# Local attention with a unit of far heads behind every two units of near heads

## The reference

```python
DSWA_CONFIGS = ((128, 1), (512, 4), (2048, 16))
...
def banded_attention(q, k, v, bias, half):
...
    s = jnp.einsum('nbqhe,nbkhe->nbhqk', qb, kw).astype(jnp.float32) * (E ** -0.5)
    s = s + bias[None, None]
...
    s = jnp.where(valid[None, :, None], s, NEG_INF)
    m = jnp.max(s, axis=-1, keepdims=True)
    lse = m + jnp.log(jnp.sum(jnp.exp(s - m), axis=-1, keepdims=True))
    p = jnp.exp(s - lse)
    o = jnp.einsum('nbhqk,nbkhe->nbqhe', p.astype(v.dtype), vw).reshape(N, lp, H, E)[:, :L]
```

## Time and profile before

| | |
|---|---|
| median of 3 runs | 3214.66 us (3212.36 to 3215.52) |
| the profiled execution, its time | 3219.06 us |
| its span | 3217.3 us |
| busy share of the span | PE 94%, PEld 76%, DVE 52%, ACT 34%, POOL 37% |
| mean granted clock of TensorE | 0.967 of full speed |
| the windows stage in the trace | first matmul at 1059.05 us, last copy ends at 1126.70 us: 67.65 us, 2.1% of the span |
| the blending stage behind it | from 1127.48 us |

### The profile page before, as it was taken

The page is one execution under the profiler, slowest core; times in us unless marked ns, Lnnn a source line. Parts: engine busy times, 40 slices in busy tenths (PEclk is TensorE's granted clock), DMA queues, the critical chain, the costliest instruction groups (busy, mean ns, idle before and its releaser), DMA issues. The chain is left out here.

```text
span 3217.3 us, 49457 instructions
## 1 busy us (share of the span) xinstructions
PE 3035.2 (94%) x18790; PEld 2429.6 (76%) x18790; DVE 1671.4 (52%) x2481; ACT 1092.6 (34%) x1740; POOL 1194.3 (37%) x603
## 2 busy tenths in 40 slices
PE   8978988999999889999898999999999979999998
PEld 6855767888878677888487788888888545589987
DVE  7755654321131535311676766555556666478731
ACT  4423433222231632122321342222233435345632
POOL 3432213444444034444122032222323147646643
PEclk9989989999999989999899999999999989999999
DMA  4216453322223022222212111111111112122222
GB/s 147 91 67 233 151 169 115 102 95 94 98 93 117 13 72 96 94 98 95 84 60 74 34 58 63 65 59 65 59 66 59 51 37 50 39 79 93 109 95 85
DMA packets 80058, 275.47 MB, mean 86 GB/s; under 512 B 9484, under 2 KB 12236, under 8 KB 79147
## 3 DMA queue, kind: packets, MB, share of 16 engines
q1 hardware_dynamic: 79627, 273.21, 25.5%
q10 hardware_dynamic: 288, 0.30, 0.0%
HBM read 263.48 MB, written 2.12 MB: 83 GB/s over the span
## 5 line engine op out<-in xcount | busy, mean ns | idle before, releaser
L223 POOL TENSOR_TENSOR weights_low<-weight_ring,weights_high 128x1024 fp32r<-128x1024 f32 x329 | 828.6, 2519 | 1486.5 <-ACT weights_high L217 1422.5
L217 ACT ACTIVATE weights_high<-weight_ring 128x1024 fp32r<-128x1024 f32 x343 | 361.5, 1054 | 784.0 <-PE bank L302 759.0
L300 PE MATMUL bank<-ffn_in_high,weights_low 128*128 128x512 f32 (+2 forms) x1144 | 388.5, 340 | 1.8 <-POOL weights_low L223 1.4
L301 PE MATMUL bank<-ffn_in_low,weights_high 128*128 128x512 f32 (+2 forms) x1144 | 388.2, 339 | 0.0
L302 PE MATMUL bank<-ffn_in_high,weights_high 128*128 128x512 f32 (+2 forms) x1144 | 388.0, 339 | 0.0
L300 PEld LDWEIGHTS bank<-ffn_in_high,weights_low 128*128 128x128 f32 x1144 | 216.5, 189 | 27.1 <-POOL weights_low L223 1.6
L301 PEld LDWEIGHTS bank<-ffn_in_low,weights_high 128*128 128x128 f32 x1144 | 216.5, 189 | 24.2
L302 PEld LDWEIGHTS bank<-ffn_in_high,weights_high 128*128 128x128 f32 x1144 | 215.6, 188 | 23.8
L713 DVE TENSOR_TENSOR mlp_down_low<-mlp_hidden,mlp_down_high 128x512 fp32r<-128x512 f32 x64 | 48.2, 756 | 284.9 <-ACT mlp_down_high L632 284.7
L300 PE MATMUL bank<-mlp_down_high,weights_low 128*128 128x512 f32 x496 | 192.9, 389 | 0.0
L301 PE MATMUL bank<-mlp_down_low,weights_high 128*128 128x512 f32 x496 | 192.9, 389 | 0.0
(11 more groups left out here) (769 smaller groups left out, 7214.3 us busy)
## 6 DMA issues: line engine op xcount, KB each, us to landing
weight_ring<-in_mod SPq DMA_DIRECT2D x96, 512.0 KB, 4.8
weight_ring<-in_ffn_up SPq DMA_DIRECT2D x88, 512.0 KB, 3.3
weight_ring<-in_mlp_up SPq DMA_DIRECT2D x64, 512.0 KB, 3.2
weight_ring<-in_mlp_down SPq DMA_DIRECT2D x64, 512.0 KB, 3.2
weight_ring<-in_ffn_down SPq DMA_DIRECT2D x44, 512.0 KB, 3.3
weight_ring<-in_gdn_in SPq DMA_DIRECT2D x32, 512.0 KB, 3.2
weight_ring<-in_dswa_in SPq DMA_DIRECT2D x27, 512.0 KB, 3.2
weight_ring<-in_fh_in SPq DMA_DIRECT2D x16, 512.0 KB, 3.2
```

What stands on the lines that cost most here:

```text
L217: act.activation(self.high[:, (g.s0 + at) % SPLIT, 0:g.floats], raw, ACT.Copy).then_inc(self.high_ready, 1)
L223: pool.tensor_tensor(self.low[:, slot, 0:g.floats], self.ring[:, (g.c0 + at) % RING, 0:g.floats], self.high[:, slot, 0:g.floats], ALU.subt ...
L300: pe.matmul(bank, wl, ah, start=start, stop=False)
L301: pe.matmul(bank, wh, al, start=False, stop=False)
```

## The change

The list of units is built in another order: two near units, then one far unit, six times over. The first group is (0,0,0), (0,0,1), (1,0), the last is (0,2,2), (0,2,3), (2,2). The list of tiles follows the order in which units first use them, where before it was written out.

```diff
-    units = [(0, i, qb) for i in range(GT) for qb in range(4)] + [(gi, i, None) for gi in (1, 2) for i in range(GT)]
+    near, far = [(0, i, qb) for i in range(GT) for qb in range(4)], [(gi, i, None) for gi in (1, 2) for i in range(GT)]
+    units = [unit for n, one in enumerate(far) for unit in (*near[2 * n:2 * n + 2], one)]
     U = len(units)
-    tiles = [(gi, i) for gi in range(3) for i in range(GT)]
+    tiles = list(dict.fromkeys(unit[:2] for unit in units))
```

## The result

The changed kernel takes 3220.47 us in the median of 19 runs (3217.40 to 3225.05), where the kernel before took 3213.42 in 19 runs beside it. The ratio is 1.0017, with a 95% interval of 1.0011 to 1.0023. It is slower by 5.5 us by the ratio (3.5 to 7.4) and 7.05 us by the medians. A second comparison of the same two kernels gave 1.0016 (1.0008 to 1.0025).

The account below looks back on a forecast made before the run. TensorE was taken as bound, full in the stage's middle and idle only at its ends. Order 5.4 plus clock 1.1 made +6.5 us on the 3214.66 median: 3221.2 us, with 8 in 10 from 3216 to 3228.

Parts of the forecast that it names:

- No work added or removed: In the stage: the change adds and removes no instruction; each engine's work and the bytes moved stay.
- The waits: TensorE ahead of far turns waits for ScalarE's copy behind the far exp: 0.8 and 1.85 us alternately, 2.7 at the first.
- The chain between far scores: From one far unit's scores to the next through VectorE, ScalarE and TensorE: 10.3 us, or 10.8 with the 384-wide neighbour.
- The stage at full clock: The changed stage: start 2.0, middle 53.0 and end 13.3 us, together 68.3.
- The end: From the sixth far unit's scores to the stage's last out copy: 13.3 us.
- The old order at full clock: The stage before the change, 67.65 us less 4.7 of low-clock loss: 62.95, so the order alone costs 5.4.
- The clock: TensorE's low-clock loss in the stage: the old 4.7 us kept, plus 1.1 for two chances in three of another low stretch.
- the clock gives back 3.1 us: Rival: far scores fill the stage's old start gap, keeping full clock; 5.4 - 3.1 = +2.3 us, 3217.0; 26%.
- The rival that was not slower: Near and far units fill each other's gaps, no wait if the far exp were 1.85 us shorter or earlier: 3209.6 us; 7%.
- Low clock in half of the groups: Rival: TensorE's clock low in half of the stage's groups or more, +9 on 5.4: +14 us, 3229, up to 3238; 12%.
- the forecast's border between slower and the same: For the whole kernel, 0.2% (6.4 us) from no change, at 3221.1 us, right at the forecast.
- the 18 us: If transposes don't count as busy for TensorE's clock: low in most groups, about +18 us on top of 5.4; small chance.

Follow-up runs that it names:

- e2: The old order (near units, then far) with each far exp as one 512-column instruction per head, parts of maxima and sums left out: 3210.68 us, ratio 0.9986.
- e10: The changed kernel run again unaltered, beside the kernel before on the same chip: 3220.90 us against 3214.95, ratio 1.0016.
- e11: The changed kernel plus unused identity transposes filling TensorE's wait ahead of all six far turns: 3218.58 us, ratio 1.0011 to the kernel before.
- e1: The changed kernel with each far exp as one 512-column instruction per head, parts of maxima and sums left out: 3208.15 us, ratio 0.9980 to the kernel before.
- e4: On top of e3, ScalarE does each unit's exp one unit later: 3212.48 us, ratio 0.9994 to the kernel before.
- e3: The changed kernel with the turn three units behind the scores instead of two, weighing four, four score slots: 3221.32 us, ratio 1.0019 to the kernel before.
- e5: The changed kernel with units ordered 8 near, 6 far, 4 near: 3211.13 us, ratio 0.9984 to the kernel before.
- e6: The changed kernel plus 20 unused identity transposes ahead of the first far turn: 3217.38 us, ratio 1.0009 to the kernel before.

## Why the prediction was right

- **No work added or removed.** TensorE ran 504 matmul records in the stage in both profiles, ScalarE 190 and VectorE 90. Right.
- **The waits.** Forecast 0.8 and 1.85 us in turn and 2.7 at the first; measured 0.89, 1.67, 0.89, 1.66 and 2.52. The sums of TensorE's list were off by 0.1 to 0.2, the mechanism right.
- **The chain between far scores.** Forecast 10.3 and 10.8 us, measured 10.38 and 10.80 at full clock, with the links as forecast.
- **The stage at full clock.** Forecast 68.3; 68.27 and 68.29 in the two runs that kept full clock. The end was forecast at 13.3 and took 13.22. The old order at full clock was put at 62.95. No run had exactly this, but it can be put together from stretches at full clock: e2's start up to the first far scores (25.85 us), from there to the last turn as in the kernel before (1087.83 to 1119.63, 31.80 us), and e2's end from its last turn on (5.51 us). That makes 63.2. The order's own cost is thus 5.1 us, forecast 5.4.
- **The clock** was the term that was mis-sized. I kept the old loss of 4.7 us and added 1.1. The changed kernel lost 2.8 in its profile and 3.7 in its second one, where 5.8 was forecast. The profile of before lost 4.5 (67.65 less 63.2), which is why the two profiled stages differ by only 3.4 us. I took its loss as the usual one. That execution was 4.4 us above its median, and two of three profiles with this start kept the clock there. An estimate from the medians says the same: 5.1 for the order plus 2.3 of low clock in the changed kernel (e10 less e11) less the 5.5 to 7.05 measured leaves 0.4 to 1.9 us of low clock for the kernel before. So the loss was put too high for both kernels, and the two errors cancel in the difference: +6.5 forecast, +7.05 by the medians, 5.5 by the ratio. That the total came out this close is in part luck. It also lies at the forecast's border between slower and the same: the ratio's interval lies above 1, so the kernel is slower, but it takes in the 0.2% of that border.
- **The rivals.** That the clock gives back 3.1 us was half right at the first waits, as the place of the loss moved from 1065 to behind the first far turn and did not vanish. The rival that was not slower named the far exp as the point of decision, and e1 shows the sign changing there: with 1.43 us the new order wins. Low clock in half of the groups did come in part: it touched two of the five distances between far scores in the first profile, and three and the stage's end in the second. But it cost 2.8 and 3.7 us and not 9, since each time only the turn and the weighing behind the wait ran slow, for 1.2 to 1.6 us of loss (at the end one weighing, 0.9), and the far scores behind them took their 2.25 us of full clock again. The rival had the whole chain slow, at 3.6 us a group.

What stays open is how much of the difference is clock in the median execution. For the changed kernel the times give 2.3 us (0.9 to 4.3), for the kernel before no run measures it.

## What to carry to other kernels

Mixing long and short units in this software pipeline helped only where the long step of one engine was covered by what the others had queued until they needed its result (e1 and e4, not the change itself). Count the work between a unit's first step and the step that waits, in the new order, and compare it with the chain through the engine that is in order. When a wait names a short instruction as releaser, look at what stands ahead of that instruction on its engine: here more lookahead at the waiting end only moved the wait (e3), while starting the long step without its own wait removed it (e4). The best order tried has the long units side by side, with short ones at the pipeline's start and end (e5).

## What the runs showed of the hardware

Transposes can stand in for other matmuls where idle time would cost the clock. With 2.4 us of nothing but transposes in the first wait (e6), and with six blocks of 0.88 to 2.4 us (e11), the granted clock was 1.00 over the whole stage, where the same order without them shows 0.95 and 0.90, with low clock behind that wait both times. The Trainium skill ("TensorE: Matmul & The Clock Gate", Part 4: PE-mode transpose) says that a transpose in that mode doesn't count as busy for the clock in the same way. The fp32 transposes of these two runs do not bear this out; their records don't say in which mode they ran. Nor did the 18 us come that the prediction worked out by this rule: low clock cost the changed kernel 2.8 and 3.7 us.

An exp with a row sum costs ScalarE, from start to start, 0.385 us for 128 columns (3.08 for eight) and 0.72 for 512 (1.43 for two). The four short ones that the residue classes need thus take 1.54 us where one long one takes 0.72.
